# Latent attention: paired value products on both column halves, one fused logit instruction, triangular storage

## The reference, cut to what matters

```python
def mla_branch(h, w_in, q_norm, kv_norm, w_uq, w_ukv, w_out):
    c_q, c_kv, k_rope, z = jnp.split(h @ w_in, [...], axis=-1)
    q = (rmsnorm(c_q, q_norm) @ w_uq).reshape(bsz, L, MLA_HEADS, MLA_NOPE + MLA_ROPE)    # 16 heads, 64 + 32
    kv = (rmsnorm(c_kv, kv_norm) @ w_ukv).reshape(bsz, L, MLA_HEADS, MLA_NOPE + MLA_V)   # 64 + 64
    ...
    o = causal_block_attention(q, k, kv[..., MLA_NOPE:])   # softmax of q k^T / sqrt(96) under the causal mask, times v
    return (o.reshape(bsz, L, MLA_WIDTH) * jax.nn.silu(z)) @ w_out
```

## Time and profile before

| what | value |
|---|---|
| median of 3 runs | 2066.5 us |
| the profiled execution | 2067.48 us |
| its span in the trace | 2065.7 us (1.78 us lie around it) |
| latent attention stage, first logit product to last value product | 1648.6 to 1804.6 us |
| first transposes of head 0 to the end of the stage | 1659.9 to 1804.6 us |
| mean granted TensorE clock over the span | 0.973 of full speed |

### The profile page before, as it was taken

The page is one execution under the profiler, slowest core; times in us unless marked ns, Lnnn a source line. Parts: engine busy times, 40 slices in busy tenths (PEclk is TensorE's granted clock), DMA queues, the critical chain, the costliest instruction groups (busy, mean ns, idle before and its releaser), DMA issues.

```text
span 2065.7 us, 25536 instructions
## 1 busy us (share of the span) xinstructions
PE 1947.3 (94%) x9856; PEld 1546.0 (75%) x9856; DVE 1324.2 (64%) x2035; ACT 896.2 (43%) x1430; POOL 517.5 (25%) x511
## 2 busy tenths in 40 slices
PE   7998888999999999999999999998989999989988
PEld 5786675888757888868888877777777766578867
DVE  7997875846729446456566844767557477738373
ACT  5445546411159313432242344435544555535332
POOL 0571110466238614024221611013101211100000
PEclk9999889999999999999999999999999999999999
DMA  4335331243422535625535925311133410023311
GB/s 161 98 133 156 114 111 56 84 153 137 136 82 92 163 107 160 213 62 156 190 95 151 209 88 126 88 62 42 52 102 93 127 41 31 31 82 122 102 62 62
DMA packets 71305, 223.70 MB, mean 108 GB/s; under 512 B 17153, under 2 KB 17841, under 8 KB 70161
## 3 DMA queue, kind: packets, MB, share of 16 engines
q1 hardware_dynamic: 43488, 159.40, 23.6%
q0 software_dynamic: 24240, 55.79, 9.8%
q10 hardware_dynamic: 3456, 6.87, 1.3%
HBM read 204.80 MB, written 14.81 MB: 106 GB/s over the span
## 4 chain that ended last, share of the span: by engine, by line
PE 68%; DVE 8%; ACT 5%; issue 3%; DVEq 0%; ACTq 0%
PE bank L486 19%; PE bank L487 19%; PE bank L488 19%; PE bank L485 2%; PE bank L3501 1%; ACT swa_s L3362 1%; PE bank L3469 1%; DVE ring_low L448 1%; ACT ring_high L443 1%; PE bank L621 1%; PE bank L2871 1%; DVE swa_s L3280 1%; PE bank L2160 1%; DVE lru_x L2074 1%; PE bank L3486 1%
## 5 line engine op out<-in xcount | busy, mean ns | idle before, releaser
L448 DVE TENSOR_TENSOR ring_low<-ring,ring_high 128x1024 fp32r<-128x1024 f32 x265 | 365.0, 1388 | 348.0 <-ACT ring_high L443 347.6
L486 PE MATMUL bank<-h_high,ring_high 128*128 128x512 f32 x1240 | 504.7, 407 | 36.4 <-DVE h_low L1542 12.1
L443 ACT ACTIVATE ring_high<-ring 128x1024 fp32r<-128x1024 f32 x283 | 297.1, 1056 | 541.0 <-PE bank L488 534.8
L487 PE MATMUL bank<-h_low,ring_high 128*128 128x512 f32 x1240 | 491.7, 396 | 0.0
L488 PE MATMUL bank<-h_high,ring_low 128*128 128x512 f32 x1240 | 491.0, 396 | 0.0
L486 PEld LDWEIGHTS bank<-h_high,ring_high 128*128 128x128 f32 x1240 | 238.4, 192 | 102.7 <-issue 41.6
L487 PEld LDWEIGHTS bank<-h_low,ring_high 128*128 128x128 f32 x1240 | 238.5, 192 | 52.8 <-issue 4.3
L488 PEld LDWEIGHTS bank<-h_high,ring_low 128*128 128x128 f32 x1240 | 238.2, 192 | 51.2
L448 POOL TENSOR_TENSOR ring_low<-ring,ring_high 128x1024 fp32r<-128x1024 f32 x18 | 53.7, 2984 | 287.0 <-ACT ring_high L443 287.0
L486 PE MATMUL bank<-gated_high,ring_high 128*128 128x512 f32 x192 | 76.5, 399 | 1.4 <-DVE gated_low L3079 1.1
L488 PE MATMUL bank<-gated_high,ring_low 128*128 128x512 f32 x192 | 74.8, 390 | 0.0
(11 more groups left out here) (553 smaller groups left out, 3918.4 us busy)
## 6 DMA issues: line engine op xcount, KB each, us to landing
ring<-slabs SPq DMA_DIRECT2D x292, 512.0 KB, 3.3
acs_rows<-acs_rows POOLq DMA_DIRECT2D x16, 512.0 KB, 4.2
s_outputs<-s_ca POOLq DMA_DIRECT2D x4, 1152.0 KB, 6.7
x<-xT SPq DMA_DIRECT2D x2, 2048.0 KB, 7.7
exp_acs<-acs_rows POOLq DMA_DIRECT2D x16, 256.0 KB, 9.2
s_b<-s_br POOLq DMA_DIRECT2D x8, 512.0 KB, 4.2
s_rows<-s_powers POOLq DMA_DIRECT2D x16, 256.0 KB, 7.0
s_inputs<-s_w POOLq DMA_DIRECT2D x8, 512.0 KB, 4.1
```

What stands on the lines that cost most here:

```text
L443: act.activation(self.ring_high[:, self.splits_before[s] % AHEAD, :], self.ring[:, s % RING, :], ACT.Copy)\
L448: dve.tensor_tensor(self.ring_low[:, s % RING, :], self.ring[:, s % RING, :], self.ring_high[:, self.splits_before[s] % AHEAD, :].bitcast( ...
L486: pe.matmul(out, w[0], x[0], start=start, stop=False)
L487: pe.matmul(out, w[0], x[1], start=False, stop=False)
```

## The change

Three things change, all in the latent attention.

1. The value products of an even head are no longer in its own step. In the odd step h, PE runs those of heads h-1 and h in turn: key block 0 of both, then block 1 of both, and so on. Each head still writes its own half of bank 7. `mla_pt` gets a slot for each of the two heads, so ACT and DVE wait, before their copies, for the value products of the pair before (`pvd`), and do so in both steps.
2. `logits` becomes four `tensor_tensor_reduce` instructions, one for each row block: (bank + mask) * scale goes to `mla_s`, and its minimum to `mla_st`. The scale is now negative (the root's factor is -96**-0.5), so this minimum is the negated row maximum. The semaphore `mx` is gone: ACT waits until the bank has been read, and its exponential takes scale=-1.
3. `mla_s` and `mla_pt` hold the triangles only: 1280 columns for a head in place of 2048.

```diff
@@ stage_mla
+    logit_at = [P * i * (i + 1) // 2 for i in range(TC)]
+    prob_at = [sum(T - P * k for k in range(kt)) for kt in range(TC)]
+    def block_row(h, i):
+        return L.S[:, h % 2, logit_at[i]:logit_at[i] + (i + 1) * P]
+    def key_block(h, kt):
+        return L.PT[h % 2][:, prob_at[kt]:prob_at[kt] + T - kt * P]
...
@@ PE
-                u = ob[h // 2]
-                if h % 2 == 0:
+                if h % 2:
+                    u = ob[h // 2]
                     C.open(pe, u)
-                e = h % 2
-                for kt in range(TC):
-                    C.read(pe, pb[h][kt])
-                    mm = pe.matmul(C.bank[u.b][64 * e:64 * e + 64, kt * P:T], L.V[:, kt, 64 * h:64 * h + 64],
-                                   L.PT[:, kt, kt * P:T], start=(kt == 0), stop=(kt == TC - 1))
-                mm.then_inc(pvd.sem, 1)
-                if e:
+                    for kt in range(TC):
+                        for g in (h - 1, h):
+                            C.read(pe, pb[g][kt])
+                            e = g % 2
+                            mm = pe.matmul(C.bank[u.b][64 * e:64 * e + 64, kt * P:T], L.V[:, kt, 64 * g:64 * g + 64],
+                                           key_block(g, kt), start=(kt == 0), stop=(kt == TC - 1))
+                            if kt == TC - 1:
+                                mm.then_inc(pvd.sem, 1)
                     pe.wait_ge(pvd.sem, pvd.at(h))
                     pe.sem_inc(C.bank_full[u.b], 1)
@@ DVE
-                    dve.scalar_tensor_tensor(out=L.S[:, h % 2, i, 0:w], in0=C.bank[u.b][:, 0:w], scalar=C.st[:, 1, i:i + 1],
-                                             in1=L.MB[:, T - w:T], op0=ALU.mult, op1=ALU.add).then_inc(C.bank_read[u.b], 1)
-                for i, u in enumerate(sb[h]):
-                    C.read(dve, u)
-                    ln(dve.tensor_reduce(st[:, 0, i:i + 1], L.S[:, h % 2, i, 0:(i + 1) * P], AX.X, ALU.max))
-                    dve.tensor_scalar(st[:, 0, i:i + 1], st[:, 0, i:i + 1], -1.0, None, ALU.mult).then_inc(mx.sem, 1)
+                    dve.tensor_tensor_reduce(out=block_row(h, i), in0=C.bank[u.b][:, 0:w], in1=L.MB[:, T - w:T],
+                                             scale=C.st[:, 1, i:i + 1], scalar=LARGEST, op0=ALU.add, op1=ALU.min,
+                                             accum_out=st[:, 0, i:i + 1]).then_inc(C.bank_read[u.b], 1)
...
+                if h > 1:
+                    dve.wait_ge(pvd.sem, pvd.at(h - h % 2 - 1))
@@ ACT
-                for i in range(TC):
-                    act.wait_ge(mx.sem, mx.at(TC * h + i))
-                    ins = act.activation(s, s, ACT.Exp, bias=st[:, 0, i:i + 1], accum_out=st[:, 1, i:i + 1])
+                for i, u in enumerate(sb[h]):
+                    C.read(act, u)
+                    ins = act.activation(s, s, ACT.Exp, scale=-1.0, bias=st[:, 0, i:i + 1], accum_out=st[:, 1, i:i + 1])
...
-                if h > 0:
-                    act.wait_ge(pvd.sem, pvd.at(h - 1))
+                if h > 1:
+                    act.wait_ge(pvd.sem, pvd.at(h - h % 2 - 1))
@@ stage_mla_latents
-            qn.token_root_on_dve(dve, 96 ** -0.5)
+            qn.token_root_on_dve(dve, -96 ** -0.5)
@@ branch_mla
-    L.S = C.at("mla_s", [P, 2, TC, T], A + 58 * KB)
+    L.S = C.at("mla_s", [P, 2, 1280], A + 58 * KB)
-    L.PT = C.at("mla_pt", [P, TC, T], C.SQ_OFF)
+    L.PT = [C.at(f"mla_pt{e}", [P, 1280], at) for e, at in enumerate((C.SQ_OFF, A + 68 * KB))]
```

More of the change, by code:

```diff
@@ L42 @@
 C_GATE = C_Q + DM
+LARGEST = 3.0e38
 NEG = -1e30
@@ L3451, in stage_mla @@
     C.pinned = ()
-    mx, ex, pn = C.reserve("mx", TC * H), C.reserve("ex", H), C.reserve("pn", H)
+    ex, pn = C.reserve("ex", H), C.reserve("pn", H)
     kt_, pvd, scd = C.reserve("ktile", 2 * 8 + 4), C.reserve("pvd", H), C.reserve("scd", H)
@@ L3485, in _ @@
                     for i in range(kt, TC):
-                        mm = pe.transpose(C.bank[u.b][:, i * P:(i + 1) * P], L.S[:, h % 2, i, kt * P:(kt + 1) * P], C.ident[:])
+                        mm = pe.transpose(C.bank[u.b][:, i * P:(i + 1) * P], block_row(h, i)[:, kt * P:(kt + 1) * P], C.ident[:])
                     mm.then_inc(C.bank_full[u.b], 1)
@@ L3530, in probs @@
                 for i in range(TC):
-                    s = L.S[:, h % 2, i, 0:(i + 1) * P]
+                    s = block_row(h, i)
                     ins = dve.tensor_scalar(s, s, st[:, 1, i:i + 1], None, ALU.mult)
@@ L3561, in _ @@
                     C.full(dve, u)
-                    dve.tensor_copy(L.PT[:, kt, kt * P:T], C.bank[u.b][:, kt * P:T]).then_inc(C.bank_read[u.b], 1)
+                    dve.tensor_copy(key_block(h, kt), C.bank[u.b][:, kt * P:T]).then_inc(C.bank_read[u.b], 1)
                 if h + 1 < H:
@@ L3631, in _ @@
                     C.full(act, u)
-                    act.activation(L.PT[:, kt, kt * P:T], C.bank[u.b][:, kt * P:T], ACT.Copy).then_inc(C.bank_read[u.b], 1)
+                    act.activation(key_block(h, kt), C.bank[u.b][:, kt * P:T], ACT.Copy).then_inc(C.bank_read[u.b], 1)
                 if h + 2 < H:
```

## The result

| what | before | after |
|---|---|---|
| median of 4 runs each, taken side by side | 2066.61 us (2065.87 to 2069.48) | 2051.99 us (2048.77 to 2054.84) |
| the profiled execution | 2067.48 us | 2048.77 us |
| first transposes (head 0) to last value product | 144.38 us | 128.09 us |

What follows compares the result with a forecast made beforehand. PE was taken to set the pace, DVE not far behind. Savings of 12.4 us in six pairs, 2.3 in the first step and 0.3 in the last window made 15.0: median 2051.5 us, own range 2046.5 to 2055.5.

Steps and rivals of the forecast that it cites:

- Value products in turn: Value products on PE: the two column halves overlap, so a pair of heads takes 2.3 us, not 4.61; saves 2.3.
- The fused instruction: Logits on DVE: scale, mask, copy and maximum in one cost 2.3 us per head; DVE loses 4.3 us a pair.
- What was late next: Odd step: the fourth logits product waits for ACT's copy, costing PE 0.57 us; about half the even logits' 0.32 wait goes.
- The long pairs: Two windows of about 20.0 us, where ACT has one more slab: forecast 17.6 us each; regular pairs 17.0.
- Half of 1.1: Long windows: about half of a 1.1 us wait on ACT goes.
- Next to no slack: DVE and ACT path: keys end at 9.2, even transposes at 9.3, so any lateness goes one for one into seven pairs.
- The first step: Start of the stage: head 0's value products come off this step, saving 2.3 us; its 2.07 us wait stays.
- The end: Last window, 15.49 us, bound by DVE: products end at 15.2, a gain of 0.3 us.
- The collision with POOL: Odd step: POOL's low part overlaps DVE's four multiplications, taking 3.40 us instead of 1.27; costs PE nothing.
- The wait chain: Rival, chance 0.18: a dearer fused instruction or later ACT delays exponentials, keys and even logits; 2056 to 2064 us.
- No overlap: Rival, chance 0.05: a pair's value products still take 4.6 us; 2063.5 us, or 2081 with weight loads in the open.
- a dear instruction: Rival, chance 0.05: at the reciprocal's 8.4 us per head a pair takes 27.3 us; 2121 us.

Runs made afterwards that it cites:

- all orders: Changed kernel with ACT's odd-step copies earlier, key slab's high part after the next even step's copies, head 15's probabilities scaled before the gated output: 2046.2 us.
- one half after the other: Changed kernel with all value products of head h-1, then all of head h, still in the odd step, without alternation: 2057.8 us.
- copies first: Changed kernel with ACT's odd-step copies of transposed blocks ahead of the slab's high part, tanh and gated high part: 2051.8 us.

## Why the prediction was right, point by point

The time, the sign and the mechanism came out. Two terms were off and partly cancelled: the stage lost 16.3 us where the sum said 15.0, with 2.4 more than forecast in the six pairs and 1.2 less at the end. That the median (2051.99) lay within half a microsecond of the forecast is luck: the same kernel run again gave 2049.9.

**Value products in turn: right.** A pair's products take 2.35 us, 2.3 was taken from the other stages' rows; turning the turns off cost 9.1 us. The loads' mean is 143 ns, 16 of them 2.3 us, and all are covered: the two halves' loads run side by side, and beside products in flight. The rule of the Trainium skill (TensorE: Matmul & The Clock Gate, Part 3), that only a load for another row group overlaps, does not hold for this pair of column halves: it would have added the loads to 2.35.

**The fused instruction: right.** 31.5/16 + 5.1/16 = 2.29 us a head, 2.3 predicted; from the first's start to the last's end it is 2.0 (1774.63 to 1776.59 in step 13), because the accumulator reads overlap. As the Trainium skill says (VectorE: DVE Perf Modes, Two Vector instructions with no wait between them), a second instruction reads the accumulator; the trace agrees, at 79 ns. That the fused instruction brings the exponentials forward and takes waits from PE is shown by the kernel with that part alone.

**What was late next: right in place and size.** ACT's tanh, gated high part and copy hold the fourth odd logits product, as predicted. Transposes and logits take 3.8 us (to 1706.67), where 4.0 was predicted and 3.40 stood before. One part was not in the working: the transposes no longer follow 64-column products but 128-column ones and take 1.09 instead of 1.24 (all orders); no run separates the width from what else changed ahead of them. With transposes of 1.09 and logits of 2.16 the wait itself is 0.55, for 0.57 predicted. The even logits' wait went wholly (0.32), not by half. Together 16.75 instead of 17.0.

**The long pairs: too cautious.** "Half of 1.1" was to stay; 0.2 of it did. With the slack just measured this reads well: exponentials come two microseconds earlier, more than the long pairs' lateness. The six pairs lost 14.8 us (115.67 to 100.90), 12.4 predicted. "Next to no slack" was wrong for regular pairs, by 1.0 us, and right for long ones.

**The first step: right,** 2.40 for 2.3.

**The end: wrong sign.** "That gives 0.3 us" became 0.88 more. The 0.3 was itself a slip: it set 15.2, where the products end, against a window of 15.49 that holds the 0.29 us hand-over behind them, so the working really gave nothing. The step that failed is the last of its working, "transposes and first copy 12.6, products 15.2". The DVE part of it held: the multiplications ended at 1780.76, 10.7 us after 1770.10, where 11.2 was taken. But from there the last products ended after 5.3 us, not 4.0. The working priced them at full clock. Before, PE had value products to do between its waits, of which the longest was 1.83 us; now both heads' products come last, PE has only the transposes of head 14 to do (1.28 us), then idles 2.99 us, and the transposes and products that follow run at a granted clock of 0.68. The kernels with a shorter idle time there, 0.38 and 1.43 us and, one half after the other, 1.98, keep the clock at 1.00, and their transposes take 1.31; in every kernel with 2.50 us or more it fell. How much it fell does not follow the idle time (0.53 after 2.54 us, 0.68 after 2.99), and why is open.

**The collision with POOL: right,** free in regular pairs (low parts on DVE), though not at the end: with all orders it stretched head 14's multiplications by 2.1 us (by 1.6 in the changed kernel) and, through the clock, cost 1.5 more.

**The rivals.** The wait chain is real, but the fused instruction's price kept it away: 1.86 us a head more gives back 10.05 us of the stage (138.14 less 128.09), where the working had 12.6 for 1.8 in seven pairs. No overlap and a dear instruction were ruled out by the rows of the result.

What stays open: the spread of the work ahead of the stage, 1645 to 1654 us for the same code; what the triangles bring, taken as nothing and never run alone (ACT's exponentials stay at a mean of 561 ns and DVE's copies at 419); and the size of the clock's fall at the end.

## What to carry to other kernels

When two engines each bound a step by little, price a saving on one together with the one on the other: here the parts bring 5.7 and 2.5 us alone and 16.3 together. Work that was moved may have been the cover of something else; list what ran beside it, find which wait shows up in its place, and reorder that engine's own work so that what the bound engine needs comes first. One such order alone can bring nothing (copies first) and pay only with the others. At the end of a stage, count PE's idle time after the move, and price what follows at the clock that such an idle time leaves.

## What the runs showed of the hardware

- Two column halves with different stationary operands overlap fully in turns (2.35 us for what took 4.61), and in part without turns (3.87).
- A `tensor_tensor_reduce` on DVE with these operands costs what the same pass without the reduction costs (542 and 543 ns), and its accumulator read (79 ns) runs beside the next instruction.
- PE's granted clock, 2.4 GHz in the stage, went in part to 1.2 GHz (mean 0.68 over the next 5.3 us) after 2.50 and 2.99 us of idle time at the end, and stayed at 1.00 after 0.38, 1.43 and 1.98. In the kernel before it had stayed at 1.00 there.
- POOL's pass over a slab stretches DVE's multiplications from SBUF to SBUF from 1.27 to 2.85 us for four (3.38 where it starts in their middle), and their mean from 383 to 613 ns.
